# A 2-layer streaming encoder step: the first norm by sums over loaded rows of x, applied while its modulation loads

## The chip, the core and the metric

The kernel runs on one core of a Trainium2 chip. A core has TensorE (PE in the profile: matrix products, transpositions), VectorE (DVE), ScalarE (ACT: function tables, scaled copies), GpSimd (POOL) and SyncE (SP), which here issues most loads. Each engine works through its own queue in order, and they wait for each other by semaphores. The metric is the device time of one execution in microseconds (us). All data is fp32.

## What is computed

A two-layer trunk over 256 prompt rows and 8 x 16 sample rows of width 1024 (384 rows together), conditioned by c, of which there are 9 rows (1 prompt, 8 samples). Cut to what matters here:

```
def rmsnorm(x, g):
    y = xf * lax.rsqrt(jnp.mean(xf * xf, axis=-1, keepdims=True) + EPS)
    return (y * g.astype(jnp.float32)).astype(x.dtype)
...
    for l in range(DEPTH):
        mod = (jax.nn.silu(c) @ w_ada[l] + b_ada[l]).reshape(c.shape[0], N_MOD, D_MODEL)[:, :, None, :]
        h = rmsnorm(x, norm_g[l, 0]) * (1.0 + mod[:, 1]) + mod[:, 0]
        x = x + FFN_RES * mod[:, 2] * rmsnorm(swiglu(h, ffn_w_in[l, 0], ffn_w_out[l, 0]), norm_g[l, 1])
        ...
        h, st = token_mixing(h, pos, past, w_in[l], b_forget[l], w_branch[l], w_out[l])
        ...
```

`swiglu(h)` is `(silu(h @ w_gate) * (h @ w_up)) @ w_down`; token mixing holds three attention branches. The change touches only the first `h` of layer 0.

## The kernel before

x is held turned: X and H are 128 partitions (a block of 128 channels) x 8 blocks (k) x 384 rows. Columns 0 to 255 are prompt rows, 256 to 383 sample rows. The rows are worked on as two groups of 192 (group 0 or "a", group 1 or "b").

At the start SP loads x as rows (QR), c and the identity (IDENT), the raw biases and norm gains (BGR), then the first four modulation weights ADA_FIRST (2 MB each: 256 columns of shift and 256 of scale, so two blocks k of H each) and with them the "quarters" of the first SwiGLU tile XIN (0.5 MB each: two blocks k of 512 columns), then constants (masks, rotary tables), then the first two tiles of the ring RING (L417; each waits for a modulation product that frees its place).

PE turns x with 24 transpositions in 6 groups (L652) through two PSUM banks; ACT copies each group into X (L1361). ACT and DVE form silu(c) in BIG (L1358, L1851), PE turns it (L657), DVE copies it to CT (L1853). ACT squares X (L1371, 16 instructions), DVE adds the squares of the 8 blocks (L1867, 14), and a matmul with ONES (L663, function `mean`) gives every partition the sum of each row; ACT makes the reciprocal root from it by Ln and Exp (L1377, L1378).

The first modulation and the first product are four stages (`first_quarters` on PE, `first_norm` on DVE, `modulate_prompt` on ACT). In stage a: PE multiplies CT with ADA_FIRST[a] (L669, `ada_unit`), DVE copies the sums to AR (L1926), PE transposes AR (L676, `ada_turned`), DVE adds the bias (L2167), forms the scale (L2172), multiplies X with the norm and, for sample columns, with scale and shift (L2176 to L2184), and ACT scales and shifts the prompt columns (L1387). `quarter(q)` multiplies H's blocks 2q and 2q+1 with quarter q of XIN (L693, 8 matmuls); PE runs quarter(a-1) behind modulation a. Its sums feed the first two of 22 column tiles of the SwiGLU; the others follow as one long run (L727), for which DVE forms sums of weights and of H. Nothing else sets the order: it is written out in each engine's program.

Of the kernel before, what the change touches and what calls it, by code (L numbers as in the profile page):

```python
# [21 lines left out]
P = 128  # L22
# [139 lines left out]
def program(nc, t):  # L162
    with ExitStack() as ctx:
# [73 lines left out]
        BGR = [big(8192 + i * P, P) for i in range(DEPTH)]  # L237
        XIN = QKTR[:, 0:KD * 512].rearrange("p (k w) -> p k w", w=512)
# [72 lines left out]
        in_x, in_c, in_k, in_id = sem("in_x"), sem("in_c"), sem("in_k"), sem("in_id")  # L311
        c_act, c_silu, c_ready, ct_ready = sem("c_act"), sem("c_silu"), sem("c_ready"), sem("ct_ready")
        xt_ready, xt_free, x_turned = sem("xt_ready"), sem("xt_free"), sem("x_turned")
# [26 lines left out]
        bf_full, gc_full, gn_full = sem("bf_full"), sem("gc_full"), sem("gn_full")  # L340
# [23 lines left out]
        out_ready, out_stored = sem("out_ready"), sem("out_stored")  # L364
# [33 lines left out]
        def _(sp):  # L398
            sp.dma_start(qr(0, 2048).rearrange("p (t d) -> p t d", t=2),
                         t["x_prompt"].rearrange("o (t p) d -> p (o t) d", p=P)).then_inc(in_x, 16)  # L400
            sp.dma_start(qr(2048, 1024), t["x_sample"].rearrange("b t d -> (b t) d")).then_inc(in_x, 16)
            sp.dma_start(BIG[0:1, 0:D], t["c_prompt"]).then_inc(in_c, 16)
            sp.dma_start(BIG[1:NC, 0:D], t["c_sample"]).then_inc(in_c, 16)
            sp.dma_start(IDENT[:, :], t["k_ident"]).then_inc(in_id, 16)
            for l in range(DEPTH):
                sp.dma_start(BGR[l][0:72, :], t["b_ada"][l].rearrange("(m p) -> m p", p=P)).then_inc(bg_full, 16)
                sp.dma_start(BGR[l][72:120, :], t["norm_g"][l].rearrange("n (k p) -> (n k) p", p=P)).then_inc(bg_full, 16)

# [112 lines left out]
            sp.dma_start(MASKS, t["k_masks"]).then_inc(in_k, 16)  # L521
# [2030 lines left out]
```

## Time and profile before

| | us |
|---|---|
| median of 3 runs | 2334.58 |
| lowest, highest | 2334.51, 2334.95 |
| profiled execution, its time | 2335.47 |
| profiled execution, its span | 2333.6 |

The span runs from the first to the last recorded instruction; the rest of the execution's time lies around it. Engines' shares of the span: PE 98% (its weight loads 88%), DVE 53%, ACT 24%, POOL 0%. DMA moved 390.10 MB. All of it comes from one profiled execution. A wait in it is named by the engine that sat idle and by what released it; a time "from the start" is from the start of the span. An fp32 matmul that is not a transposition leaves two records.

### The profile page before, as it was taken

What the parts mean: (1) busy time and instruction counts of PE and PEld (TensorE: products, weight loads), DVE (VectorE), ACT (ScalarE), POOL (GpSimd) and SP (SyncE); (2) the same over time, 40 slices, a digit from 0 to 9 for tenths busy, and PEclk for the clock granted to TensorE, in tenths of its full rate; (3) what the DMA queues carried; (4) which work ended last, traced back from release to release, by engine and by line L of the source; (5) the groups of instructions that cost most, each with busy time, mean ns of one, the idle gap of its engine ahead of it and who ended that gap; (6) DMA issues with size and microseconds to landing.
All of it is one profiled execution on the core that took longest, in us unless ns stands there. A gap on an engine that the chain in (4) does not pass through costs nothing.

```text
span 2333.6 us, 41217 instructions
## 1 busy us (share of the span) xinstructions
PE 2297.0 (98%) x16916; PEld 2049.9 (88%) x16916; DVE 1231.9 (53%) x2700; ACT 556.3 (24%) x1349; POOL 68.8 (3%) x112
## 2 busy tenths in 40 slices
PE   7999999999999999999999999999999999999998
PEld 5999997886688699999999999978856886999998
DVE  5566433543656446666275664426345754666742
ACT  3000113113564231001130010321235642400011
POOL 0000000000022000000000000000000220000000
PEclk9999999999999999999999999999999999999999
DMA  9455234783489453443435533447825984233232
GB/s 337 136 176 176 96 127 152 232 263 103 149 286 343 138 191 111 145 145 100 136 127 178 177 131 116 167 132 237 261 68 189 333 290 149 73 109 109 100 122 77
DMA packets 300509, 390.10 MB, mean 167 GB/s; under 512 B 31005, under 2 KB 251033, under 8 KB 300322
## 3 DMA queue, kind: packets, MB, share of 16 engines
q1 hardware_dynamic: 281090, 336.41, 42.9%
q0 software_dynamic: 11712, 42.18, 5.2%
q10 hardware_dynamic: 7520, 8.87, 1.1%
q8 instruction: 135, 2.21, 0.4%
q14 instruction: 52, 0.43, 0.1%
HBM read 375.30 MB, written 12.12 MB: 166 GB/s over the span
## 4 chain that ended last, share of the span: by engine, by line
PE 94%; DMA 2%; ACT 2%; SPq 1%; DVE 1%; issue 1%; ACTq 0%; DVEq 0%
PE PS L727 31%; PE PS L823 13%; PE PS L1013 6%; PE PS L961 4%; PE PS L1281 4%; PE PS L910 4%; PE PS L669 3%; PE PS L1099 3%; PE PS L1180 3%; PE PS L871 2%; PE PS L983 2%; PE PS L879 2%; PE PS L1313 2%; PE PS L1321 2%; PE PS L1220 2%; PE PS L1195 1%
## 5 line engine op out<-in xcount | busy, mean ns | idle before, releaser
L727 PE MATMUL PS<-OT,RING 128*128 128x192 f32 x1280 | 234.1, 326 | 0.0
L727 PE MATMUL PS<-H,RING 128*128 128x192 f32 x1280 | 222.1, 327 | 0.0
L727 PE MATMUL PS<-OT,QR 128*128 128x192 f32 x1280 | 221.1, 326 | 0.0
L727 PEld LDWEIGHTS PS<-OT,RING 128*128 128x128 f32 x1280 | 212.4, 190 | 0.0
L727 PEld LDWEIGHTS PS<-H,RING 128*128 128x128 f32 x1280 | 208.4, 190 | 3.8 <-issue 3.2
L727 PEld LDWEIGHTS PS<-OT,QR 128*128 128x128 f32 x1280 | 210.2, 190 | 0.0
L1425 ACT ACTIVATE QR<-QR 128x384 f32<-128x384 f32 x80 | 41.8, 522 | 533.8 <-DVE QR L2011 533.8
L1013 PE MATMUL PS<-H,RING 128*128 128x384 f32 x480 | 161.1, 490 | 0.0
L1013 PEld LDWEIGHTS PS<-H,RING 128*128 128x128 f32 x480 | 88.9, 190 | 60.2 <-issue 3.7
L727 PE MATMUL PS<-H,QR 128*128 128x192 f32 x640 | 117.1, 326 | 0.0
L1867 DVE TENSOR_TENSOR OT<-OT 128x192 f32<-128x192 f32 x168 | 57.7, 354 | 105.7 <-ACT OT L1396 93.6
L727 PEld LDWEIGHTS PS<-H,QR 128*128 128x128 f32 x640 | 106.2, 190 | 0.0
L2011 DVE TENSOR_TENSOR QR<-PS,QR 128x384 f32<-128x384 f32 x80 | 44.6, 557 | 111.0 <-PE PS L727 111.0
L1281 PE MATMUL PS<-OT,RING 128*128 128x384 f32 x288 | 94.4, 487 | 0.0
L910 PE MATMUL PS<-RING,H 128*128 128x384 f32 (+1 forms) x288 | 90.3, 471 | 0.0
L823 PE MATMUL PS<-BIG,RING 128*128 128x192 f32 x528 | 89.7, 326 | 0.0
L2063 DVE TENSOR_TENSOR QR<-RING 128x768 f32<-128x768 f32 (+1 forms) x24 | 21.4, 890 | 124.3 <-DMA RING<-ffn_w_out 124.3
L823 PEld LDWEIGHTS PS<-BIG,RING 128*128 128x128 f32 x528 | 86.5, 190 | 0.0
L2006 DVE TENSOR_TENSOR QR<-PS,QR 128x384 f32<-128x384 f32 x80 | 44.4, 555 | 79.6 <-PE PS L727 79.6
L1281 PEld LDWEIGHTS PS<-OT,RING 128*128 128x128 f32 x288 | 54.1, 190 | 36.1
L910 PEld LDWEIGHTS PS<-RING,H 128*128 128x128 f32 x288 | 54.2, 190 | 32.2 <-issue 0.8
L983 PE MATMUL PS<-RING,H 128*128 128x384 f32 x224 | 74.5, 486 | 0.0
(325 smaller groups left out, 4005.7 us busy)
## 6 DMA issues: line engine op xcount, KB each, us to landing
RING<-ffn_w_in SPq DMA_DIRECT2D x80, 1024.0 KB, 7.2
RING<-w_in SPq DMA_DIRECT2D x64, 768.0 KB, 6.4
QR<-w_ada SPq DMA_DIRECT2D x34, 1024.0 KB, 9.7
BIG<-w_ada SPq DMA_DIRECT2D x34, 1024.0 KB, 10.6
RING<-ffn_w_out SPq DMA_DIRECT2D x32, 768.0 KB, 4.7
RING<-ffn_w_out SPq DMA_DIRECT2D x32, 640.0 KB, 5.4
QR<-cache_sb_v POOLq DMA_DIRECT2D x16, 768.0 KB, 5.3
QKT<-cache_sb_k SPq DMA_DIRECT2D x16, 768.0 KB, 5.7
```

The source lines that it names most:

```text
L669: mm = pe.matmul(PS[32 * j:32 * j + 32, bank, col:col + P], CT[:, k, :], w[:, k, j * P:(j + 1) * P], start=(k == 0), stop=(k == KD - 1))
L727: mm = pe.matmul(PS[:, bank, GROUP[g]], a[:, k, :], x[:, k, :], start=(k == 0), stop=(k == 3))
L823: mm = pe.matmul(PS[:, bank, 0:HALF], a[:, k, :], x[:, k, :], start=(half == 0 and k == 0), stop=(half == 1 and k == kn - 1))
L871: mm = pe.matmul(PS[:, m, 0:HALF], w[:, k, m * P:(m + 1) * P], HID[:, half * k2 + k, GROUP[0]], start=(half == 0 and k == 0), stop=(half = ...
L910: mm = pe.matmul(PS[:, n % 3, 0:width], H[:, k, tt * P:(tt + 1) * P], w[:, k, :], start=(k == 0), stop=(k == KD - 1))
L961: mm = pe.matmul(PS[:, bank, GROUP[half]], a[:, k, :], x[:, k, :], start=(k == 0), stop=(k == 3))
L983: mm = pe.matmul(PS[:, 4, 0:MIX], H[:, k, 2 * P:T], w[:, k, :], start=(k == 0), stop=(k == KD - 1))
L1013: mm = pe.matmul(PS[:, bank, 0:T], w[:, k, (n % 3) * P:(n % 3 + 1) * P], H[:, k, :], start=(k == 0), stop=(k == KD - 1))
L1099: mm = pe.transpose(PS[:, bank, c * P:(c + 1) * P], KC[:, n % KBUF, c, a * P:(a + 1) * P], IDENT[:, :])
L1180: mm = pe.matmul(PS[:, 3, 0:HALF], w[:, k, (n % 3) * P:(n % 3 + 1) * P], H[:, k, GROUP[half]], start=(k == 0), stop=(k == KD - 1))
L1281: mm = pe.matmul(PS[:, 3 * (m % 2) + n, 0:T], w[:, 3 * n + k, m * P:(m + 1) * P], OT[:, 3 * n + k, :], start=(k == 0), stop=(k == NPAIR - 1))
L1867: V.tensor_tensor(SQ[:, 0, GROUP[g]], SQ[:, 0, GROUP[g]], SQ[:, k, GROUP[g]], ALU.add).then_inc(sq_added[g], 1)
```

## The change

- **Loads.** x comes in three loads with a semaphore each. c (now as 72 rows of 128: `C0`), the identity, the biases and gains are issued by ACT, behind its table load. The first ADA_FIRST load is split by k into halves, each with its own wait inside `ada_unit`; quarters 2 and 3 of XIN move each behind its modulation weights; the constants move behind the first two ring tiles.
- **silu(c)** is Exp on ACT, then on DVE an addition, a reciprocal and a product on 72 x 128; one transposition turns it.
- **The norm.** ACT squares the loaded rows (`Square` with a running sum over the row, three instructions of 1024 columns), makes the reciprocal root of the 384 sums in 3 columns, DVE puts them on diagonals (DIAG, 128 x 384), and one matmul with ONES spreads them over all partitions in PSUM. DVE multiplies X with that, 4 instructions of 768 columns into H, ahead of the first modulation's copy AR. The old squares, additions, means and roots of this norm go; semaphores are advanced for them.
- **Copies of turned x** go from ACT to DVE.
- **PE** runs filling matmuls `warm(n)` on ONES, and `quarter(a)` now stands behind modulation a, not a+1.
- **Stage work.** DVE multiplies and adds the sample columns only; ACT scales 256 prompt columns in one instruction per block.

The semaphores' declarations, the body of `constants()` and the moved bias transposition and copy are left out of the diff.

```diff
@@ -396,15 +401,9 @@
 
         @block.sync
         def _(sp):
-            sp.dma_start(qr(0, 2048).rearrange("p (t d) -> p t d", t=2),
-                         t["x_prompt"].rearrange("o (t p) d -> p (o t) d", p=P)).then_inc(in_x, 16)
-            sp.dma_start(qr(2048, 1024), t["x_sample"].rearrange("b t d -> (b t) d")).then_inc(in_x, 16)
-            sp.dma_start(BIG[0:1, 0:D], t["c_prompt"]).then_inc(in_c, 16)
-            sp.dma_start(BIG[1:NC, 0:D], t["c_sample"]).then_inc(in_c, 16)
-            sp.dma_start(IDENT[:, :], t["k_ident"]).then_inc(in_id, 16)
-            for l in range(DEPTH):
-                sp.dma_start(BGR[l][0:72, :], t["b_ada"][l].rearrange("(m p) -> m p", p=P)).then_inc(bg_full, 16)
-                sp.dma_start(BGR[l][72:120, :], t["norm_g"][l].rearrange("n (k p) -> (n k) p", p=P)).then_inc(bg_full, 16)
+            for i in range(2):
+                sp.dma_start(qr(i * D, D), t["x_prompt"][0, i * P:(i + 1) * P, :]).then_inc(in_x[i], 16)
+            sp.dma_start(qr(2 * D, D), t["x_sample"].rearrange("b t d -> (b t) d")).then_inc(in_x[2], 16)
...
             for a in range(N_ADA_FIRST):
-                for i in range(2):
-                    sp.dma_start(ADA_FIRST[a][:, :, i * 256:(i + 1) * 256],
-                                 w[:, :, i * D + a * 256:i * D + (a + 1) * 256]).then_inc(first_full[a], 16)
-                for q in ((0,), (1,), (), (2, 3))[a]:
+                for h in range(2 if a == 0 else 1):
+                    ks = slice(4 * h, 4 * h + 4) if a == 0 else slice(0, KD)
+                    for i in range(2):
+                        sp.dma_start(ADA_FIRST[a][:, ks, i * 256:(i + 1) * 256],
+                                     w[:, ks, i * D + a * 256:i * D + (a + 1) * 256]).then_inc(
+                                         (first_full[0], second_half)[h] if a == 0 else first_full[a], 16)
+                for q in ((0,), (1,), (2,), (3,))[a]:
                     for dst, src in ffn_in(0, 0, XIN, 0):
                         sp.dma_start(dst[:, 2 * q:2 * q + 2, :], src[:, 2 * q:2 * q + 2, :]).then_inc(quarter_full[q], 16)
...
+            def warm(n):
+
+                for _ in range(n):
+                    pe.matmul(PS[:, 7, 0:P], ONES[:, :], ONES[:, :], start=True, stop=True)
+
+            def turned_in(g):
                 pe.wait_ge(xt_free, g + 1)
                 for j in range(4):
                     k, tt = 4 * (g % 2) + j, g // 2
                     mm = pe.transpose(PS[:, g % 2, j * P:(j + 1) * P],
                                       qr(tt * 1024 + k * P, P), IDENT[:, :])
                 mm.then_inc(xt_ready, 1)
+
+            pe.wait_ge(ones_ready, 1)
+            warm(6)
+            pe.wait_ge(in_id, 16)
+            for tt in range(TT):
+                pe.wait_ge(in_x[tt], 16)
+                turned_in(2 * tt)
+                turned_in(2 * tt + 1)
             pe.wait_ge(c_ready, 1)
-            for k in range(KD):
-                mm = pe.transpose(PS[:, 2, k * NC:(k + 1) * NC], BIG[0:NC, 3 * D + k * P:3 * D + (k + 1) * P], IDENT[0:NC, 0:NC])
-            mm.then_inc(ct_ready, 1)
+            pe.transpose(PS[:, 2, 0:KD * NC], C0, IDENT[0:KD * NC, 0:KD * NC]).then_inc(ct_ready, 1)
+            pe.wait_ge(bg_full, 64)
+            for i in range(DEPTH):
+                mm = pe.transpose(PS[:, 4, i * P:i * P + 120], BGR[i][0:120, :], IDENT[0:120, 0:120])
+            mm.then_inc(bg_ready, 1)
+            warm(4)
+            pe.wait_ge(diag_ready, 1)
+            pe.matmul(PS[:, 6, 0:T], ONES[:, :], OTR[:, D:D + T], start=True, stop=True).then_inc(ms_ready[0], 1)
+            warm(8)
             pe.wait_ge(c_silu, 1)
 
             def mean(q, g):
                 pe.wait_ge(sq_added[g], 7 * q + 7)
                 pe.matmul(PS[:, 6 + g, 0:HALF], ONES[:, :], SQ[:, 0, GROUP[g]], start=True, stop=True).then_inc(ms_ready[g], 1)
 
...
-            def ada_unit(w, bank=6, col=0):
+            def ada_unit(w, bank=6, col=0, halves=None):
 
                 for k in range(KD):
+                    if halves and k % 4 == 0:
+                        pe.wait_ge(halves[k // 4], 32)
                     for j in range(4):
                         mm = pe.matmul(PS[32 * j:32 * j + 32, bank, col:col + P], CT[:, k, :], w[:, k, j * P:(j + 1) * P],
                                        start=(k == 0), stop=(k == KD - 1))
...
-                    ada_unit(ADA_FIRST[a], 3)
+                    if a:
+                        pe.wait_ge(first_full[a], 32)
+                        ada_unit(ADA_FIRST[a], 3)
+                    else:
+                        ada_unit(ADA_FIRST[a], 3, halves=(first_full[0], second_half))
                     ada_turned(a, 0)
                     if a == 0:
-                        for g in range(2):
-                            mean(0, g)
-                    else:
-                        quarter(a - 1)
-                quarter(N_ADA_FIRST - 1)
+                        warm(6)
+                    quarter(a)
                 pe.wait_ge(mod_free, N_ADA_FIRST + 1)
 
...
+            nc.scalar.preload_act_table_set("natural_log_exp_and_others")
+            act.dma_start(BIG[0:KD, 0:P], t["c_prompt"].rearrange("o (k p) -> (o k) p", p=P)).then_inc(in_c, 16)
+            act.dma_start(BIG[KD:KD * NC, 0:P], t["c_sample"].rearrange("b (k p) -> (b k) p", p=P)).then_inc(in_c, 16)
+            act.dma_start(IDENT[:, :], t["k_ident"]).then_inc(in_id, 16)
+            for l in range(DEPTH):
+                act.dma_start(BGR[l][0:72, :], t["b_ada"][l].rearrange("(m p) -> m p", p=P)).then_inc(bg_full, 16)
+                act.dma_start(BGR[l][72:120, :], t["norm_g"][l].rearrange("n (k p) -> (n k) p", p=P)).then_inc(bg_full, 16)
+            begin()
             act.wait_ge(in_c, 32)
...
+            A(C1, C0, ACT.Exp, scale=-1.0).then_inc(c_act, 1)
+            for tt in range(TT):
+                act.wait_ge(in_x[tt], 16)
+                link(A(XSQ, qr(tt * D, D), ACT.Square, accum_out=XSUM[:, tt:tt + 1]))
+            act.wait_ge(ones_ready, 1)
+            link(A(XRSTD, XSUM, ACT.Ln, scale=1.0 / D, bias=EPSC[:, :]))
+            A(XRSTD, XRSTD, ACT.Exp, scale=-0.5).then_inc(rstd_ready[0], 1)
 
             def squares_of_x(e, g, ks):
 
...
+            for k in range(KD):
+                act.wait_ge(coef_ready, k // 2 + 1)
+                act.wait_ge(hs_ready[0], k // 2 * 2 + 2)
+                h = H[:, k, 0:NPROMPT]
+                A(h, h, ACT.Identity, scale=MOD[0][:, KD + k, 0:1], bias=MOD[0][:, k, 0:1]).then_inc(h_ready[0], 1)
 
...
+            def taken_in(g):
+
+                dve.wait_ge(xt_ready, g + 1)
+                V.tensor_copy(X[:, 4 * (g % 2):4 * (g % 2) + 4, (g // 2) * P:(g // 2 + 1) * P],
+                              PS[:, g % 2, :].rearrange("p (k t) -> p k t", k=4)).then_inc(xt_free, 1)
+
+            taken_in(0)
+            taken_in(1)
             dve.wait_ge(c_act, 1)
-            c, e, g = (BIG[0:NC, i * D:(i + 1) * D] for i in (0, 1, 3))
-            V.tensor_tensor(g, c, e, ALU.mult).then_inc(c_ready, 1)
+            link(V.tensor_scalar(C2, C1, 1.0, None, ALU.add))
+            link(V.reciprocal(C1, C2))
+            V.tensor_tensor(C0, C0, C1, ALU.mult).then_inc(c_ready, 1)
+            for g in range(2, 6):
+                taken_in(g)
             dve.wait_ge(ct_ready, 1)
-            link(V.tensor_copy(CT[:, :, 0:NC], PS[:, 2, 0:KD * NC].rearrange("p (k c) -> p k c", c=NC)))
+            link(V.tensor_copy(CT[:, :, 0:NC].rearrange("p k c -> p c k"), PS[:, 2, 0:KD * NC].rearrange("p (c k) -> p c k", c=NC)))
             link(V.tensor_copy(ROWS[:, :].rearrange("p (z t) -> p z t", z=2), IDENT[:, 0:NT][:, None, :].to_broadcast([P, 2, NT])))
             dve.sem_inc(c_silu, 1)
-            dve.wait_ge(x_turned, 1)
-            for g in range(2):
-                dve.sem_inc(x_ready[g], KD)
+            dve.wait_ge(rstd_ready[0], 1)
+            V.tensor_tensor(DIAG, IDENT[:, :][:, None, :].to_broadcast([P, TT, P]), XRSTD[..., None].to_broadcast([P, TT, P]),
+                            ALU.mult).then_inc(diag_ready, 1)
+            dve.wait_ge(bg_ready, 1)
+            for i in range(DEPTH):
+                ins = V.tensor_copy(BG[i][:, :], PS[:, 4, i * P:i * P + 120])
+            ins.then_inc(bg_free, 1)
+            dve.wait_ge(xt_free, 2 + 6)
+            dve.wait_ge(ms_ready[0], 1)
+            for q in range(N_ADA_FIRST):
+                k = slice(2 * q, 2 * q + 2)
+                V.tensor_tensor(H[:, k, :], X[:, k, :], PS[:, 6, 0:T][:, None, :].to_broadcast([P, 2, T]), ALU.mult).then_inc(hs_ready[0], 2)
 
             def add_squares(q, g, ks):
...
                 dve.sem_inc(coef_ready, 1)
-                for g in range(2):
-                    dve.wait_ge(rstd_ready[g], 1)
-                link(V.tensor_tensor(sample_cols(H)[:, k], sample_cols(X)[:, k], per_sample(0, KD)[:, k], ALU.mult))
-                for i in (2 * q, 2 * q + 1):
-                    V.tensor_tensor(H[:, i, 0:HALF], X[:, i, 0:HALF], RSTD[:, 0:HALF], ALU.mult).then_inc(hs_ready[0], 1)
-                V.tensor_tensor(H[:, k, HALF:NPROMPT], X[:, k, HALF:NPROMPT],
-                                RSTD[:, HALF:NPROMPT][:, None, :].to_broadcast([P, 2, NPROMPT - HALF]), ALU.mult)
-                link(V.tensor_tensor(H[:, k, NPROMPT:T], H[:, k, NPROMPT:T],
-                                     RSTD[:, NPROMPT:T][:, None, :].to_broadcast([P, 2, NSAMPLE]), ALU.mult))
+                dve.wait_ge(hs_ready[0], 2 * q + 2)
                 hs = sample_cols(H)[:, k]
-                V.tensor_tensor(hs, hs, per_sample(0, 0)[:, k], ALU.add).then_inc(hs_ready[1], 2)
+                link(V.tensor_tensor(hs, hs, per_sample(0, KD)[:, k], ALU.mult))
+                V.tensor_tensor(hs, hs, per_sample(0, 0)[:, k], ALU.add).then_inc(h_ready[1], 2)
 
             for q in range(N_ADA_FIRST):
```

PE, from the first transposition to the second stage's quarter, before (QR holds x, BIG c and the raw biases, CT silu(c), RING and QR later modulation weights, QKT the tile XIN):

```order
L652 MATMUL PS<-IDENT,QR 128x128 x24
L657 MATMUL PS<-IDENT,BIG 128x9 x8
L892 MATMUL PS<-IDENT,BIG 128x120 x2
L669 MATMUL PS<-RING,CT 32x128 x32
L676 MATMUL PS<-IDENT,AR 128x128
L663 MATMUL PS<-OT,ONES 128x192 x2
L669 MATMUL PS<-RING,CT 32x128 x32
L676 MATMUL PS<-IDENT,AR 128x128
L693 MATMUL PS<-H,QKT 128x384 x8
```

and after:

```order
L662 MATMUL PS<-IDENT,QR 128x128 x24
L674 MATMUL PS<-IDENT,BIG 128x72
L677 MATMUL PS<-IDENT,BIG 128x120 x2
L656 MATMUL PS<-ONES 128x128 x4
L681 MATMUL PS<-OT,ONES 128x384
L656 MATMUL PS<-ONES 128x128 x8
L695 MATMUL PS<-RING,CT 32x128 x32
L702 MATMUL PS<-IDENT,AR 128x128
L656 MATMUL PS<-ONES 128x128 x6
L719 MATMUL PS<-H,QKT 128x384 x8
L695 MATMUL PS<-RING,CT 32x128 x32
```

The spreading matmul (L681) stands ahead of the first modulation product, and the first quarter ahead of the second one.

DVE, from the silu of c to the end of the first stage, before:

```order
L1851 TENSOR_TENSOR BIG<-BIG 9x1024
L1853 COPY CT<-PS 128x8x9
L1854 COPY ROWS<-IDENT 128x32
L2156 COPY BG<-PS 128x120 x2
L1867 TENSOR_TENSOR OT<-OT 128x192 x14
L1926 COPY AR<-PS 128x128
```

and after, from the first copies of turned x on:

```order
L1881 COPY X<-PS 128x4x128 x2
L1887 TENSOR_SCALAR BIG<-BIG 72x128
L1888 RECIPROCAL BIG<-BIG 72x128
L1889 TENSOR_TENSOR BIG<-BIG 72x128
L1881 COPY X<-PS 128x4x128 x4
L1893 COPY CT<-PS 128x9x8
L1894 COPY ROWS<-IDENT 128x32
L1897 TENSOR_TENSOR OT<-IDENT,ST 128x384
L1901 COPY BG<-PS 128x120 x2
L1907 TENSOR_TENSOR H<-X,PS 128x768 x4
L1975 COPY AR<-PS 128x128
```

Fourteen additions leave the place ahead of AR, and four products of 768 columns, six copies and the diagonal take it.

## Rows read from the trace of the kernel before

**Rows 1.** The page, part 1: busy us, share of the span, instructions.

```profile
PE 2297.0 (98%) x16916; PEld 2049.9 (88%) x16916; DVE 1231.9 (53%) x2700; ACT 556.3 (24%) x1349; POOL 68.8 (3%) x112
```

**Rows 2.** The page, part 4: the chain that ended last, by engine.

```profile
PE 94%; DMA 2%; ACT 2%; SPq 1%; DVE 1%; issue 1%; ACTq 0%; DVEq 0%
```

**Rows 3.** Waits of PE, 0 to 100 us: total, times, longest.

```profile
PE PS L652 <- DMA IDENT<-k_ident: 8.1, 1, 8.1
PE PS L676 <- DVE AR L1926: 5.1, 4, 3.5
```

**Rows 4.** Timeline from the start: start, us, engine, line, operation [idle before].

```profile
0.73 1.28 ACT L1358 ACT_TABLE_LOAD   x1 [0.73 <-PEq L2544]
...
2.42 0.37 SPq L404 DMA_DIRECT2D IDENT<-k_ident  x1
...
8.09 5.09 PE L652 MATMUL PS<-IDENT,QR 128*128 128x128 f32 x24 [8.09 <-DMA IDENT<-k_ident]
...
9.21 0.60 ACT L1361 ACTIVATE X<-PS 128x512 f32<-128x512 f32 x1 [0.42 <-PE PS L652]
...
13.80 0.23 DVE L1853 COPY CT<-PS 128x72 f32<-128x72 f32 x1 [3.69 <-PE PS L657]
...
14.37 0.42 PE L892 MATMUL PS<-IDENT,BIG 120*128 120x120 f32 x2 [0.60 <-DVEq L1855]
...
15.35 3.53 PE L669 MATMUL PS<-RING,CT 128*32 128x128 f32 x64 [0.56 <-DVE BG L2156]
...
22.04 0.28 DVE L1926 COPY AR<-PS 128x128 f32<-128x128 f32 x1
```

**Rows 5.** Timeline of the third stage, and where the long run begins.

```profile
33.33 1.95 PE L669 MATMUL PS<-QR,CT 128*32 128x128 f32 x64
...
35.35 0.29 DVE L1926 COPY AR<-PS 128x128 f32<-128x128 f32 x1 [4.62 <-PE PS L669]
...
35.70 0.33 PE L676 MATMUL PS<-IDENT,AR 128*128 128x128 f32 x1 [0.41 <-DVE AR L1926]
...
35.87 5.33 PE L693 MATMUL PS<-H,QKT 128*128 128x384 f32 x16
36.07 0.20 DVE L2167 TENSOR_TENSOR MOD<-PS,BG 128x36 f32<-128x36 f32 x1 [0.42 <-PE PS L676]
...
36.70 0.43 DVE L2176 TENSOR_TENSOR H<-X,MOD 128x256 f32<-128x256 f32 x1 [0.22 <-DVE MOD L2172]
...
37.61 0.98 ACT L1387 ACTIVATE H<-H,MOD 128x192 f32<-128x192 f32 x2 [6.01 <-DVE H L2178]
...
41.13 1.69 PEld L669 LDWEIGHTS PS<-BIG,CT 128*32 128x32 f32 x64 [0.55 <-issue]
...
53.99 5.36 PE L727 MATMUL PS<-H,RING 128*128 128x192 f32 x32
```

**Rows 6.** DMA issues: count, KB each, median us from issue to landing.

```profile
IDENT<-k_ident SPq DMA_DIRECT2D x1, 64.0 KB, 5.6
...
o_y_p<-QR ACTq DMA_DIRECT2D x4, 256.0 KB, 2.0
```

**Rows 7.** Groups by line and shape: busy us, mean ns | idle before.

```profile
L2420 DVE COPY NORM<-PS 128x512 f32<-128x512 f32 x24 | 16.3, 681 | 0.0
...
L1979 DVE TENSOR_TENSOR OT<-H 128x768 f32<-128x768 f32 x4 | 3.8, 951 | 0.0
...
L2428 DVE RECIPROCAL ST<-ST 128x1 f32<-128x1 f32 x24 | 3.7, 153 | 0.0
...
L2386 DVE RECIPROCAL ST<-ST 128x6 f32<-128x6 f32 x8 | 1.5, 192 | 12.3 <-ACT QR L1652 12.0
...
L1647 ACT ACTIVATE QR<-QR 128x768 f32<-128x768 f32 x4 | 3.4, 844 | 0.1
```

**Rows 8.** Windows: us, PE busy (instructions), granted clock, DMA share, GB/s.

```profile
15.00:19.00 4.00, 3.53 (x64) 0.57 1.09 386
27.00:28.00 1.00, 0.33 (x1) 1.00 1.10 354
```

More of the change, by code:

```diff
@@ L237, in program @@
         BGR = [big(8192 + i * P, P) for i in range(DEPTH)]
+        C0, C1, C2 = (BIG[0:KD * NC, i * P:(i + 1) * P] for i in range(3))
+        XSQ, DIAG = OTR[:, 0:D], OTR[:, D:D + T].rearrange("p (t c) -> p t c", t=TT)
+        XSUM, XRSTD = ST[:, 0:TT], ST[:, 8:8 + TT]
         XIN = QKTR[:, 0:KD * 512].rearrange("p (k w) -> p k w", w=512)
@@ L308, in sems @@
             return [sem(f"{name}_{g}") for g in "ab"]
-        in_x, in_c, in_k, in_id = sem("in_x"), sem("in_c"), sem("in_k"), sem("in_id")
+        in_x = [sem(f"in_x{i}") for i in range(TT)]
+        in_c, in_k, in_id = sem("in_c"), sem("in_k"), sem("in_id")
         c_act, c_silu, c_ready, ct_ready = sem("c_act"), sem("c_silu"), sem("c_ready"), sem("ct_ready")
-        xt_ready, xt_free, x_turned = sem("xt_ready"), sem("xt_free"), sem("x_turned")
+        ones_ready, diag_ready = sem("ones_ready"), sem("diag_ready")
+        xt_ready, xt_free, second_half = sem("xt_ready"), sem("xt_free"), sem("first_second_half")
         settled = sem("settled")
@@ L643, in full @@
                 pe.wait_ge(slot_full[n % 2], 32 * (n // 2 + 1))
-            pe.wait_ge(in_x, 32)
-            pe.wait_ge(in_id, 16)
-            for g in range(6):
+            def warm(n):
+                for _ in range(n):
+                    pe.matmul(PS[:, 7, 0:P], ONES[:, :], ONES[:, :], start=True, stop=True)
+            def turned_in(g):
                 pe.wait_ge(xt_free, g + 1)
@@ L888, in swiglu_out @@
                         mm.then_inc(half_used, 1)
-            pe.wait_ge(bg_full, 64)
-            for i in range(DEPTH):
-                mm = pe.transpose(PS[:, 3, i * P:i * P + 120], BGR[i][0:120, :], IDENT[0:120, 0:120])
-            mm.then_inc(bg_ready, 1)
-            pe.wait_ge(bg_free, 2)
             for l in range(DEPTH):
@@ L1383, in modulate_prompt @@
                 for k in ks:
-                    act.wait_ge(coef_ready, COEF_NORM[e] if e else k // 2 + 1)
+                    act.wait_ge(coef_ready, COEF_NORM[e])
                     act.wait_ge(hs_ready[g], 8 * e + k + 1)
@@ L1844, in _ @@
             link(V.memset(EPSC[:, :], EPS))
-            link(V.memset(ZERO[:, :], 0.0))
-            link(V.memset(QBLK, 0.0))
-            link(V.memset(CT, 0.0))
-            dve.wait_ge(c_act, 1)
-            c, e, g = (BIG[0:NC, i * D:(i + 1) * D] for i in (0, 1, 3))
-            V.tensor_tensor(g, c, e, ALU.mult).then_inc(c_ready, 1)
+            dve.sem_inc(ones_ready, 1)
+            for g in range(2):
+                for s, n in ((sq_ready[g], KD), (sq_added[g], KD - 1), (x_ready[g], KD)):
+                    dve.sem_inc(s, n)
@@ new lines, in _ @@
+            for s, n in ((ms_ready[1], 1), (rstd_ready[1], 1), (hs_ready[1], KD)):
+                dve.sem_inc(s, n)
+            link(V.memset(CT, 0.0))
+            link(V.memset(ZERO[:, :], 0.0))
+            def taken_in(g):
[3 more added lines that the diff above has]
+            taken_in(0)
@@ new lines, in _ @@
+            dve.wait_ge(bg_ready, 1)
+            for i in range(DEPTH):
+                ins = V.tensor_copy(BG[i][:, :], PS[:, 4, i * P:i * P + 120])
[5 more added lines that the diff above has]
+                V.tensor_tensor(H[:, k, :], X[:, k, :], PS[:, 6, 0:T][:, None, :].to_broadcast([P, 2, T]), ALU.mult).then_inc(hs_ready[0], 2)
@@ L2152, in choose @@
                     link(V.match_replace(WK[qt], M8, WK[qt], TAKEN))
-            dve.wait_ge(bg_ready, 1)
-            for i in range(DEPTH):
-                ins = V.tensor_copy(BG[i][:, :], PS[:, 3, i * P:i * P + 120])
-            ins.then_inc(bg_free, 1)
             dve.wait_ge(bg_free, 2)
```

40 lines of the change are left out of this document (11 added, 29 removed).

## The prediction

> **What bounds the kernel now.** I read the page first: TensorE (PE) is busy 98% of the span [rows 1], and the chain that ended last is 94% PE, 2% DMA, 2% ScalarE (ACT) [rows 2]. So the change can only matter where PE waits. The waits of the first 100 us say where that is in the edited part: 8.1 us until the identity matrix has landed, and 5.1 us in total (3.5 us the longest) for VectorE's (DVE's) copy AR [rows 3]. The timeline shows the order [rows 4]: PE turns x from 8.09, the silu of c is ready with the copy at 13.80, the first modulation product (L669, 64 records) starts at 15.35, and its copy AR only starts at 22.04, because DVE adds squares until then. From 33.33 there is no such wait; one stage is shown in [rows 5]: modulation product 33.33, AR 35.35, its transposition 35.70, and at 35.87 a quarter of the first SwiGLU product (L693), which belongs to the modulation before this one. So DVE and ACT prepare H (from 36.07 on) under that quarter, and PE is never idle for it. At 53.99 the long solid stretch (L727) begins. After that row nothing is edited that PE waits for; the change is worth what it moves 53.99, and all else shifts with it.
>
> **How long one stage becomes.** The order rows show that quarter q now stands right behind modulation q and its transposition, where before quarter q-1 stood. Everything between transposition and H is then in PE's way. From [rows 5]: the transposition starts at 35.70, the bias addition at 36.07, then the scale, and the first product with H at 36.70, so 1.00 us. That product (0.43) stays for the sample columns; the addition behind it (0.43) follows at a distance of 0.11, as for other dependent pairs on DVE; 0.1 for the semaphore: 1.00 + 0.43 + 0.11 + 0.43 + 0.1 = 2.07 us from transposition to quarter, where 0.17 stood. ACT's two modulations of 256 columns run beside it from about 0.95 on; two of 192 take 0.98 [rows 5], so they end at the same place. The products of x with the norm no longer stand here: they were DVE's and hidden; that removal is worth 0 in these stages. One stage: 2.02 (33.33 to 35.35) + 0.35 + 2.07 + 5.26 (35.87 to 41.13) = 9.70 us. Of four stages the last has no product behind it: 38.8 us from the first modulation product to L727. Before, it is 53.99 - 15.35 = 38.6 us, with the 3.5 us wait and half-clock stretches in it. So what is gained at the first wait is spent in four new ones, and **L727 moves by about what the first modulation product moves** (15.2 is the even point).
>
> **Where the first modulation product goes.** It needs its weights, c, and in PE's order now also the mean of squares and eight filling matmuls. Weights: they were there at 15.35, and the halves come no later. The rest hangs on the identity's landing I. Before: issued 2.42, landed 8.0 [rows 4, 6]. Now ACT issues it behind its table load and two loads of c, at about 2.7 (table load 0.73 + 1.28, two issues of some 0.35 as SP's). Bounds for the landing are 5.6 us and 2.0 us, the quickest landing in the trace, a store from ACT's queue at the end [rows 6]: I = 4.7 to 8.3. I take 6.3, since it stands behind no megabyte on its queue but shares the DMA engines with x.
>
> The Trainium skill, "DMA: Bandwidth & Descriptors", section "Issuing engines are not separate DMA queues", says that issues of several engines interleave on the same 16 DMA engines and that spreading them saves only issue time; this speaks against the change. No row before has two queues busy at the start. By that rule I would be 8.3, and the sum below 2.0 us more; that is rival D.
>
> From I on, DVE is the longest chain. First copy of turned x 1.1 later (8.09 to 9.21 [rows 4]); six copies of 512 from PSUM at 0.68 [rows 7] (ACT did them before) = 4.1; silu by three operations on 72x128 between the second and the third: addition 0.25, product 0.28, and a reciprocal, whose rows give 153 ns for 1 column and 192 for 6, so 7.8 ns a column and 1.14 for 128 [rows 7], with gaps 1.95 in all; waits for two banks 0.7 (four transpositions 0.8 and the way there are longer than one copy); CT 0.23 [rows 4], ROWS less than that, diagonal of 384 columns some 0.55, gaps 0.4. Together 1.1 + 8.1 = 9.2. ACT's three squares of 1024 columns (some 1.1 each, from 844 ns for 768 [rows 7]) end before that: cost 0. The bias transpositions, two, lie in PE's pauses: 0. On PE then the mean, one matmul of 384 columns, is an eighth of a quarter (5.26 us), 0.65; eight fills of 128 columns 8 x 0.215 = 1.7. First modulation product: 6.3 + 9.2 + 0.65 + 1.7 + 0.05 = **17.9**, against an even point of 15.2: **+2.7 us**. DVE's four new products of 768 columns (4 x 0.95 [rows 7], 3.75) start with the mean's end, 16.2, and end at 20.0, just as the modulation product (1.95) does: no more cost, but none to spare. What was removed here (16 squares, 14 additions, four root steps) is in the 38.6 and so counted.
>
> **The clock.** PE at half clock: from 15 to 19 the granted clock is 0.57 on average, that is at its lower level (1.2 of 2.4 GHz) for most of it, after light work (two small transpositions at 14.37, pauses on both sides [rows 4]); such a stretch costs 4 x (1 - 0.57) = 1.7 us of PE work [rows 8]. A gap of 0.7 us with one transposition (27 to 28) brought no fall [rows 8]. Start: if the mean, the fills or the modulation product fall into a stretch at half clock, up to 1.7 is added; I add 0.8: **+3.5**. Stages: each has 0.4 idle, one transposition of 0.33, then 1.74 idle (the first filled by six matmuls). That is more idle than the case that fell and less than the wait of 3.5 us. I take one fall in the three unfilled gaps: +1.7, bounds 0 and 5.1.
>
> **Other edits.** Constants of 1 MB move behind the two ring loads: used only at the projections, cost 0; the ring loads are earlier. DMA: each stage needs 2.6 MB at 354 to 386 GB/s [rows 8], 7 us in 9.7: hidden, and the split of the first load and of the quarters gives nothing once the product starts at 17.9. The memset of QBLK was under the loads: 0. ACT's second table load (1.28 [rows 4]) goes, off the path that now decides. DVE's sums behind the last quarter: four of 512 columns at about 0.7 and four of 768 at 0.95, 6.6 us, beside 5.2 us of quarter and 5 us of L727 products that need only H: hidden by 3 us.
>
> **Sum.** 2335.47 us of the profiled execution (span 2333.6) + 3.5 + 1.7 = 2340.7; the profiled execution is 0.9 over the median of 2334.58, so 2339.8 on the scale of the medians.
>
> **The rivals.**
> A, the forecast: start +3.5 and one or more falls of the clock, 2339.8 (2338.5 to 2343). For it: the gap nearest in kind fell. 0.45.
> B, no fall in the gaps: 2338.1 (2336.5 to 2339.5). For it: the gap at 27; PE is at work 7.5 of 9.7 us. 0.25.
> C, not slower: the small loads on ACT's queue land at once (I = 4.7) and the silu slips between copies that wait anyway (0.7 and 1.0 less): product at 14.6, 0.6 us under the even point, 2334.0; with the loads alone early 16.3, 2335.7. It decides from a product start below 15.2. Against it: DVE's nine copies and products in a row. 0.15.
> D, the identity waits behind x as before (I = 8.3): +5.5 without a fall, +7.2 with one: 2340.1 to 2341.8. 0.12.
> E, clearly faster: needs the product before 10.6 or a stage without its gap. The first is excluded by the weights (2.1 MB behind 1.6 MB of x) and the second by the waits for H. 0.03 for what I overlook.
>
> **How the numbers follow.** A measurement of this kernel tells 0.2% (4.7 us, above 2339.25) from no change. Slower: most of A (0.42), D 0.12 and a little of B: 0.55. Same: the rest of A, B and C: 0.42. Faster 0.03. The likeliest case gives 2339.8; the range 2335.5 to 2342.5 leaves out the early half of C, E, and starts with three falls.
>
> **What would show it.** Right: the first modulation product starts at 16.3 to 19.9; behind each of the four AR transpositions PE is idle or filling for about 1.7 us until H, released by DVE's sample addition or ACT; stages of 9.7 us; L727 from 56.7 to 61; half-clock slices behind one or two gaps; identical waits after that. The reciprocal takes about 1.1 us. Wrong: stages of 7.9 us, a product before 15, L727 before 54, or a change of more than 1 us behind L727's start.

## The result, and the profile after

| | before | changed |
|---|---|---|
| median, us | 2334.43 (7 runs, 2333.78 to 2334.95) | 2341.90 (7 runs, 2340.15 to 2343.38) |
| ratio to before, 95% interval | | 1.0030 (1.0020 to 1.0039) |
| profiled execution, time and span | 2335.47, 2333.6 | 2341.90, 2340.1 |

The change makes the kernel slower by 7.5 us. The forecast was 2339.8 with a range of 2335.5 to 2342.5, and slower with a chance of 0.55. The medians lie 7.5 us apart, the two profiled executions 6.4.

The timeline of the changed kernel up to the first quarter (start, us, engine, line, operation [idle before, what ended it]); compare [rows 4]:

```profile
2.04 0.60 ACTq L1380 DMA_DIRECT2D IDENT<-k_ident  x1
...
8.17 4.00 PE L662 MATMUL PS<-IDENT,QR 128*128 128x128 f32 x16 [2.43 <-DMA IDENT<-k_ident]
...
11.03 0.95 DVE L1888 RECIPROCAL BIG<-BIG 72x128 f32<-72x128 f32 x1
...
13.05 1.16 PE L662 MATMUL PS<-IDENT,QR 128*128 128x128 f32 x8 [0.87 <-DVE X L1881]
...
14.32 1.06 PE L656 MATMUL PS<-ONES 128*128 128x128 f32 x8
...
16.17 0.91 PE L681 MATMUL PS<-OT,ONES 128*128 128x384 f32 x2 [0.79 <-DVE OT L1897]
...
16.92 1.95 PE L656 MATMUL PS<-ONES 128*128 128x128 f32 x16
17.23 3.55 DVE L1907 TENSOR_TENSOR H<-X,PS 128x768 f32<-128x768 f32 x4 [0.73 <-PE PS L681]
18.80 1.96 PE L695 MATMUL PS<-RING,CT 128*32 128x128 f32 x64
...
21.24 0.33 PE L702 MATMUL PS<-IDENT,AR 128*128 128x128 f32 x1 [0.49 <-DVE AR L1975]
...
23.67 5.40 PE L719 MATMUL PS<-H,QKT 128*128 128x384 f32 x16 [0.76 <-DVE H L2222]
```

The 3.5 us wait for AR is gone (0.49 is left), and the first quarter starts at 23.67 where it started at 28.00. But the first modulation product starts at 18.80 where it started at 15.35. Then one stage and the start of the long run, against [rows 5]:

```profile
29.00 1.95 PE L695 MATMUL PS<-RING,CT 128*32 128x128 f32 x64
...
31.02 0.29 DVE L1975 COPY AR<-PS 128x128 f32<-128x128 f32 x1 [7.50 <-PE PS L695]
31.37 0.33 PE L702 MATMUL PS<-IDENT,AR 128*128 128x128 f32 x1 [0.41 <-DVE AR L1975]
...
32.23 1.09 ACT L1495 ACTIVATE H<-H,MOD 128x256 f32<-128x256 f32 x2 [9.03 <-DVEq L2218]
32.29 0.42 DVE L2221 TENSOR_TENSOR H<-H,MOD 128x256 f32<-128x256 f32 x1
32.83 0.42 DVE L2222 TENSOR_TENSOR H<-H,MOD 128x256 f32<-128x256 f32 x1
...
33.40 5.40 PE L719 MATMUL PS<-H,QKT 128*128 128x384 f32 x16 [1.70 <-ACT H L1495]
38.72 1.95 PE L695 MATMUL PS<-QR,CT 128*32 128x128 f32 x64
...
43.12 6.94 PE L719 MATMUL PS<-H,QKT 128*128 128x384 f32 x16 [1.70 <-ACT H L1495]
...
59.62 5.36 PE L753 MATMUL PS<-H,RING 128*128 128x192 f32 x32
```

From transposition to quarter it is 33.40 - 31.37 = 2.03 us, where 0.17 stood; a stage is 38.72 - 29.00 = 9.72 us, where it was 7.8. One quarter took 6.94 us instead of 5.40. The windows (us, PE busy, granted clock, DMA share, GB/s) say why: the granted clock fell to its lower level (1.2 GHz) for a part of the first window. Nothing of the kind came with the last gap:

```profile
42.00:47.00 5.00, 3.88 (x8) 0.66 1.09 397
51.00:54.00 3.00, 1.27 (x37) 1.00 0.23 29
```

The long run starts 5.6 us later than before. The waits of PE in the first 100 us (total, times, longest), against [rows 3]:

```profile
PE PS L719 <- ACT H L1495: 5.1, 3, 1.7
PE PS L662 <- DMA IDENT<-k_ident: 2.4, 1, 2.4
PE PS L702 <- DVE AR L1975: 1.7, 4, 0.5
```

Behind the long run's start the two traces run alike for a long way. One solid piece of PE work of 75.08 us (L823 before, L849 after), which comes back several times, starts at 249.32, 1075.25 and 1397.51 before, and at 254.94, 1080.79 and 1403.05 after, always 5.5 to 5.6 later. The missing 0.9 us up to the spans' difference of 6.5 arose after 1403, in the second layer, where nothing was edited. It need not be a cost of the change: the span behind the long run's start is 2279.6 us here before and 2280.5 after, and it was 2278.0 in a second profiled execution of the same changed kernel.

### The profile page after: what moved, and what is told of

The parts are those of the page before. It is cut to its first block, busy times and chain, and to the rows that moved or that the text cites. A ratio compares the mean times of both kernels' runs of the same rounds, so it can differ in the third digit from the quotient of the medians.

```text
span 2340.1 us, 41239 instructions
## 1 busy us (share of the span) xinstructions
PE 2302.4 (98%) x16955; PEld 2054.2 (88%) x16955; DVE 1228.0 (52%) x2682; ACT 546.8 (23%) x1322; POOL 68.8 (3%) x112
## 4 chain that ended last, share of the span: by engine, by line
PE 94%; ACT 2%; SPq 2%; DMA 1%; DVE 1%; issue 1%; ACTq 0%; DVEq 0%
PE PS L753 31%; PE PS L849 13%; PE PS L1033 6%; PE PS L1301 4%; PE PS L981 4%; PE PS L930 4%; PE PS L695 3%; PE PS L1119 3%; PE PS L1200 3%; PE PS L897 2%; PE PS L1003 2%; PE PS L905 2%; PE PS L1333 2%; PE PS L1341 2%; PE PS L1240 2%; PE PS L1215 1%
## 5 line engine op out<-in xcount | busy, mean ns | idle before, releaser
L1916 DVE TENSOR_TENSOR OT<-OT 128x192 f32<-128x192 f32 x154 | 52.7, 352 | 103.8 <-ACT OT L1423 93.6
L849 PE MATMUL PS<-BIG,RING 128*128 128x192 f32 x528 | 89.7, 326 | 0.0
L849 PEld LDWEIGHTS PS<-BIG,RING 128*128 128x128 f32 x528 | 86.5, 190 | 0.0
```

Of the source, the lines that this page charges most:

```text
L849: mm = pe.matmul(PS[:, bank, 0:HALF], a[:, k, :], x[:, k, :], start=(half == 0 and k == 0), stop=(half == 1 and k == kn - 1))
L1916: V.tensor_tensor(SQ[:, 0, GROUP[g]], SQ[:, 0, GROUP[g]], SQ[:, k, GROUP[g]], ALU.add).then_inc(sq_added[g], 1)
```

## The experiments

The first four experiments ran on one chip, the next four on a second, the last two on a third; each ratio is to runs of the kernel before on the same chip and has a 95% interval. Times are medians. Two kernels were run in two sets each; their distance to the kernel before differed by 0.6 and 1.0 us between the sets, so a difference between experiments of different sets is no finer than that.

**The order of the quarters undone.** The one edit to the changed kernel:

```diff
                     ada_turned(a, 0)
-                    if a == 0:
-                        warm(6)
-                    quarter(a)
+                    if a:
+                        quarter(a - 1)
+                quarter(N_ADA_FIRST - 1)
```

> The changed kernel with one thing undone: quarter(a-1) stands behind modulation a again, as before the change; new norm, loads and copies stay. Theory (the order exposes the way from each AR transposition to H, about 1.9 us in each of four stages, and this ate the gain of the new norm): PE has no wait for H; the first modulation product stays at 18.8 us, the first quarter comes at about 24.1, stages of 7.8 us follow, and the long run starts at about 50 us where the changed kernel has 59.6 and the one before 54.0. Time 2330.5 to 2332.5 us. Rival (the new norm and the later start of the first modulation product are what costs, the order little): long run at 57 to 58, time 2339 to 2341 us.

Measured: 2332.95 us against 2334.72, ratio 0.9991 (0.9982 to 1.0000); 9 us under the changed kernel. The profiled execution's waits for H are gone and the stage is 7.8 us again:

```profile
20.37 1.96 PE L695 MATMUL PS<-RING,CT 128*32 128x128 f32 x64
...
25.65 5.40 PE L719 MATMUL PS<-H,QKT 128*128 128x384 f32 x16
30.98 1.95 PE L695 MATMUL PS<-QR,CT 128*32 128x128 f32 x64
33.35 0.33 PE L702 MATMUL PS<-IDENT,AR 128*128 128x128 f32 x1 [0.41 <-DVE AR L1975]
33.51 5.33 PE L719 MATMUL PS<-H,QKT 128*128 128x384 f32 x16
38.78 1.96 PE L695 MATMUL PS<-BIG,CT 128*32 128x128 f32 x64
...
51.64 5.36 PE L753 MATMUL PS<-H,RING 128*128 128x192 f32 x32
```

The start of this execution was late by itself: the identity landed at 9.0 and the work up to the product took 0.7 us longer, so the first modulation product started at 20.37, not 18.80, and the long run at 51.64 instead of 50. (The changed kernel's second profile, below, has the same late start.) From first modulation product to long run it is 31.3 us, where the changed kernel has 40.8 (39.3 without its fall of the clock) and the one before 38.6. So the order alone costs 8 us, and the rival that gave it little has fallen. What else was edited makes the kernel 1.8 us faster than before at the most likely, and the interval reaches 1.0000. The time is 0.5 us above the expected range; this execution also lost 3.5 us to before between 247 and 1076 us, 1.6 of it in a single longer wait for a later modulation weight (2.0 instead of 0.4); the rest I can't place.

**The order alone.** The kernel before, with one edit:

```diff
                         for g in range(2):
                             mean(0, g)
-                    else:
-                        quarter(a - 1)
-                quarter(N_ADA_FIRST - 1)
+                    quarter(a)
```

> The kernel before with one thing changed: quarter(a) stands behind modulation a, all else as before. Theory (exposed way to H): here the products of x with the norm and the 64-column modulations stand in that way too, so it is about 4.0 us a stage (35.70 to 39.72 in the trace of before, and 0.1); first quarter at 28.3, stages of 11.8, long run at about 68.7 instead of 54.0: 2349 us, up to 2354 if the clock falls in each gap. Rival (order costs little): 2334 to 2337 us.

Measured: 2357.19 us, ratio 1.0095 (1.0080 to 1.0111), 22 us slower and 3 above the range. The last two stages:

```profile
51.11 0.33 PE L676 MATMUL PS<-IDENT,AR 128*128 128x128 f32 x1 [0.41 <-DVE AR L1924]
54.94 7.90 PE L693 MATMUL PS<-H,QKT 128*128 128x384 f32 x16 [3.51 <-ACT H L1385]
62.77 1.95 PE L669 MATMUL PS<-BIG,CT 128*32 128x128 f32 x64
65.14 0.33 PE L676 MATMUL PS<-IDENT,AR 128*128 128x128 f32 x1 [0.41 <-DVE AR L1924]
...
75.90 4.39 PE L725 MATMUL PS<-H,RING 128*128 128x192 f32 x26
```

The exposed way is 54.94 - 51.11 = 3.83 us a stage (4.0 expected). Without falls the long run would start at 27.73 + 3 x 11.5 + 5.2 = 67.4; it started at 75.90. Of the 8.5 us between them 8.3 are the clock's (stage: 1.96 + 0.41 + 3.83 + 5.3 = 11.5): the four quarters took 7.85, 7.09, 7.90 and 7.09 us instead of 5.40. So behind a gap of 3.8 us every quarter ran partly at half clock, and a fall cost up to 2.5 us, not 1.7 at most. With the new norm the order costs 9 us, with the old one 22. Read the other way, the new norm, loads and fills together save 15 us in the new order (2357.2 to 2341.9) and under 2 in the old one (2334.7 to 2333.0), where the work that they take out of the stages was hidden.

**Fills in every gap.** Six filling matmuls stand behind each AR transposition, not behind the first alone:

```diff
                     ada_turned(a, 0)
-                    if a == 0:
-                        warm(6)
+                    warm(6)
                     quarter(a)
```

> The changed kernel with the six filling matmuls (about 1.3 us of PE work) behind the AR transposition of every stage, not of the first alone. Theory (one fall of the clock in some runs' gaps, none in others, two in others): no slice at half clock between 21 us and the long run, which starts at about 58.0 instead of 59.6; median about 2340.3 us, and the runs lie within about 1.3 us of each other where the changed kernel's lie within 3.2. Rival (the spread and the level have another cause): median 2341.9 and a spread of 3 us as before, or longer where the fills are themselves late for H.

Measured: 2340.52 us, ratio 1.0025 (1.0016 to 1.0034). The median came out as expected, though the interval overlaps the changed kernel's. The profiled execution has no slice below full clock in the stages. Its long run starts at 59.85, not at 58.0, because the first modulation product started only at 20.56; from product to long run it is 39.3 us, as in the changed kernel without its fall. The spread did not shrink: 11 runs lie between 2337.8 and 2344.2, and 21 runs of the kernel before on this chip between 2333.3 and 2337.7. So the spread is not that of the falls. The profiles show two other sources, the start (product at 18.80 to 20.56) and the waits far behind it; how much each gives was not measured. The gap itself stays, now filled:

```profile
42.86 0.33 PE L702 MATMUL PS<-IDENT,AR 128*128 128x128 f32 x1 [0.41 <-DVE AR L1974]
43.02 1.50 PE L656 MATMUL PS<-ONES 128*128 128x128 f32 x12
44.89 5.40 PE L719 MATMUL PS<-H,QKT 128*128 128x384 f32 x16 [0.36 <-ACT H L1494]
```

**No fills at all.** All 24 filling matmuls of the changed kernel are left out:

```diff
-            pe.wait_ge(ones_ready, 1)
-            warm(6)
...
-            warm(4)
...
-            warm(8)
...
-                    if a == 0:
-                        warm(6)
```

> The changed kernel without any filling matmul. Theory (DVE's chain of the six copies, the silu and the four norm products sets the first AR copy at 20.9, the eight fills ahead of the first modulation product cost nothing beyond it, but keep the clock up): the product starts at about 17.1, AR at 20.9 at full clock or 21.5 to 22 at half clock, and gaps fall as often or oftener; 2341.5 to 2345 us. Rival (the fills themselves stand in the way): 1.7 us faster, 2340.2.

Measured: 2345.62 us, ratio 1.0044 (1.0031 to 1.0056), 0.6 above the range and 3.7 us slower than with them; the rival has fallen. In the profiled execution the identity landed at 8.2 as in the changed kernel's first profile. The first modulation product starts a microsecond earlier than there and ends later, because it runs at 1.2 GHz, and two of the four quarters meet a fall, the first among them, whose six fills are gone too:

```profile
17.80 3.64 PE L691 MATMUL PS<-RING,CT 128*32 128x128 f32 x64
21.94 0.48 PE L698 MATMUL PS<-IDENT,AR 128*128 128x128 f32 x1 [0.49 <-DVE AR L1969]
24.51 7.09 PE L715 MATMUL PS<-H,QKT 128*128 128x384 f32 x16 [2.09 <-DVE H L2216]
```

**The changed kernel again, and with the identity first.** The second of the two has the identity as SyncE's first load:

```diff
         def _(sp):
+            sp.dma_start(IDENT[:, :], t["k_ident"]).then_inc(in_id, 16)
...
-            act.dma_start(IDENT[:, :], t["k_ident"]).then_inc(in_id, 16)
```

> The changed kernel once more, nothing edited, as the measure for the next run on the same chip. The identity (issued on ScalarE's queue at 2.0 us) lands at 8 to 9 us, the first modulation product starts at 18.8 to 19.7, one or two falls of the clock in the three unfilled gaps: 2340 to 2343 us.

Measured: 2341.78 us, ratio 1.0029 (1.0018 to 1.0040): the result again, in another set of runs. Its profile differs from the first in three places:

```profile
8.82 4.01 PE L662 MATMUL PS<-IDENT,QR 128*128 128x128 f32 x16 [3.08 <-DMA IDENT<-k_ident]
13.70 1.94 PE L662 MATMUL PS<-IDENT,QR 128*128 128x128 f32 x8 [0.87 <-DVE X L1881]
...
15.95 1.93 PE L656 MATMUL PS<-ONES 128*128 128x128 f32 x8
...
20.41 1.96 PE L695 MATMUL PS<-RING,CT 128*32 128x128 f32 x64
...
35.00 7.09 PE L719 MATMUL PS<-H,QKT 128*128 128x384 f32 x16 [1.70 <-ACT H L1495]
...
61.38 5.36 PE L753 MATMUL PS<-H,RING 128*128 128x192 f32 x32
```

The identity landed 0.65 us later. The last transpositions of x took 1.94 us instead of 1.16 and the four fills 1.93 instead of 1.06, so PE was still at 1.2 GHz there, where in the first profile it was at 2.4 GHz from 13 us on (the windows print a granted clock of 1.00 here; the trace has no clock record ahead of the first rise, and the durations decide). From the landing to the first modulation product it is 1.0 us more for it (11.6 instead of 10.6). That product therefore starts at 20.41, 0.7 above the expected 19.7, and the long run 7.4 us later than before the change, not 5.6. The fall of the clock stands in another gap, ahead of the second quarter instead of the third. Three of the four profiles of kernels with this start have the product at 20.4 to 20.6 (the first experiment, the third and this one), so the first profile was an early one. Why the clock rises late in them is not shown.

> The changed kernel with the identity as SyncE's first load, ahead of x, instead of ScalarE's third. Theory (small loads on ScalarE's queue share the DMA engines with x and land as late as behind it; the identity's landing starts the whole chain): the first transposition waits for x's first rows instead, at about 5.6 us, the first modulation product and the long run are 2 to 2.5 us earlier than in the changed kernel, time lower by as much, 2339.5 us. Rival (the chain hangs on the silu of c, which lands at 6.9, or on the last rows of x): less than 1 us.

Measured: 2338.04 us, ratio 1.0015 (1.0006 to 1.0025), 3.7 us faster than the changed kernel beside it. PE's first transposition follows the fills without a wait for the identity:

```profile
0.74 0.39 SPq L404 DMA_DIRECT2D IDENT<-k_ident  x1
...
5.53 1.22 PE L663 MATMUL PS<-IDENT,QR 128*128 128x128 f32 x8
...
15.65 1.95 PE L696 MATMUL PS<-RING,CT 128*32 128x128 f32 x64
```

The identity landed 1.8 us after its issue. The modulation product starts at 15.65, 4.8 us earlier than in the profile of the changed kernel beside it and 3.2 earlier than in the first one; the long run starts at 56.62 instead of 61.38. So the chain hung on the identity, and more than the expected 2 to 2.5 us; the rival (less than 1 us) has fallen. Even so the kernel is 3.2 us slower than before: with the product at its old place, the exposed gaps and one fall are left.

**Norm products spread.** On top of the old order: in DVE's program one norm product stands ahead of the first AR copy, and each other behind the coefficients of the stage before; the eight fills ahead of the first modulation product are gone.

```diff
-            for q in range(N_ADA_FIRST):
+            def normed(q):
+
                 k = slice(2 * q, 2 * q + 2)
                 V.tensor_tensor(H[:, k, :], X[:, k, :], PS[:, 6, 0:T][:, None, :].to_broadcast([P, 2, T]), ALU.mult).then_inc(hs_ready[0], 2)
+
+            normed(0)
...
                 ada_rows(q, 3)
                 first_norm(q)
+                if q + 1 < N_ADA_FIRST:
+                    normed(q + 1)
```

> The old order of quarters as in the first experiment, and in addition the norm's four products of 768 columns spread: the first ahead of the first AR copy, each other behind the coefficients of the stage before; the eight fills ahead of the first modulation product are left out. Theory (DVE's 3.5 us of products and the 1.7 us of fills are what stands between the mean and AR): AR transposition 1.8 us earlier (17.5 to 19.5 us at full clock against 21.2), long run at 48.5 to 50.5: 2331 us, 1.8 below the first experiment's; if the clock falls at the start, up to 1.7 of it is lost. Rival (the start is bound by the identity alone): as the first experiment, 2333.

Measured: 2331.26 us, ratio 0.9984 (0.9975 to 0.9992). It is faster than before by 3.6 us and than the first experiment by 1.7, as expected, but on another chip and with intervals that overlap. In the profiles the first AR transposition comes at 21.17 instead of 22.81 (17.5 to 19.5 was expected; the identity landed at 8.7 and the clock rose late here too), and the long run at 50.37 instead of 51.64. So the theory agrees with the traces, while the times alone do not show the gain; the spread products and the missing fills were not tried apart.

**Both together.** The kernel with spread norm products, and the identity as SyncE's first load, by the edits shown above.

> The kernel of the run before with the identity as SyncE's first load. Theory: both gains add, the long run at 46 to 48, 2328 to 2329.5 us, 5 to 6.5 below the kernel before. Rival (the DMA is then what is late: modulation weights of the second and third stage are waited for): 2330 to 2331.

Measured: 2333.87 us, ratio 0.9996 (0.9987 to 1.0005). It is 2.6 us slower than the run before, against the theory and beyond the rival, whose mechanism it shows:

```profile
16.76 0.33 PE L702 MATMUL PS<-IDENT,AR 128*128 128x128 f32 x1 [0.49 <-DVE AR L1977]
...
21.81 3.64 PE L695 MATMUL PS<-RING,CT 128*32 128x128 f32 x64 [4.72 <-DMA RING<-w_ada]
...
52.06 4.23 PE L753 MATMUL PS<-H,RING 128*128 128x192 f32 x25
```

The first modulation product starts at 14.31, 4.4 us earlier than in the run before. PE is ready for the second one at 17.1 and waits 4.7 us for its weights, until 21.81; in the run before that product started at 21.43 without a wait. So the weights arrive when they did, and the gain at the front is lost. Behind the wait the clock was at 1.2 GHz (granted 0.62 on average from 17 to 26 us), and the product took 3.64 us instead of 1.95; these 1.7 us are what the long run starts later (52.06 against 50.37).

**A version that uses that wait.** The kernel of "Both together" with `quarter(0)` right behind modulation 0 (six fills between), the others one stage behind, four fills behind the second transposition, and XIN's second quarter loaded behind the third modulation weights, its third with its fourth. The kernel with the norm products spread ran again beside it. The edit is shown against the changed kernel, without what is shown above:

```diff
-                for q in ((0,), (1,), (2,), (3,))[a]:
+                for q in ((0,), (), (1,), (2, 3))[a]:
...
                     if a == 0:
                         warm(6)
-                    quarter(a)
+                        quarter(0)
+                    if a == 1:
+                        warm(4)
+                    if a > 1:
+                        quarter(a - 1)
+                quarter(N_ADA_FIRST - 1)
```

> The kernel of the seventh experiment (old order, norm products spread, no eight fills) once more, nothing edited, as the measure for the next run on the same chip: 2330.5 to 2332 us, the long run at about 50.4 us.

Measured: 2332.14 us, ratio 0.9989 (0.9980 to 0.9998): 0.1 above the expected range, the long run at 49.92, and 2.6 us below the kernel before where it was 3.6 the first time. Over the first experiment (1.8 below) little of the gain is left.

> The kernel of the eighth experiment (identity first, norm products spread) with the first quarter right behind modulation 0, six fills between them, where PE waited 4.7 us for the second modulation weights, and the other quarters one stage behind as in the old order; four fills behind the second AR transposition; the second quarter's load stands behind the third modulation weights. Theory (an exposed gap to H costs nothing where PE would wait for weights anyway): first quarter at 18.8 us, second modulation product at 24.1 at full clock, third at 27.5 to 28.5 when its weights have landed, long run at 48.5 to 49.2: 1.2 to 1.9 us below the seventh experiment, 2329.3 to 2330. Rival (the third weights land later, or the clock falls behind the second transposition): no gain over the seventh.

Measured: 2329.74 us, ratio 0.9975 (0.9966 to 0.9985): 5.0 us below the kernel before, 2.4 below the run beside it and 12 below the change; both the time and the long run's start are as the theory has them. Its start:

```profile
14.88 1.96 PE L695 MATMUL PS<-RING,CT 128*32 128x128 f32 x64
...
19.35 5.40 PE L719 MATMUL PS<-H,QKT 128*128 128x384 f32 x16 [0.36 <-ACT H L1499]
24.68 1.96 PE L695 MATMUL PS<-RING,CT 128*32 128x128 f32 x64
...
48.86 5.36 PE L758 MATMUL PS<-H,RING 128*128 128x192 f32 x32
```

The first quarter and the gap ahead of it cost little here: they fill the time in which the version under "Both together" waited 4.7 us for the second weights, and that wait is gone.

## Why the prediction was right

**What bounds, and what the change is worth.** Right. The spans differ by 6.5 us, and 5.6 of it is the shift of the long run's start.

**The length of a stage.** Right nearly to the digit: 2.03 us from transposition to quarter (2.07 forecast), 9.72 a stage (9.70), and in both profiles. In the first stage it was 2.43, because DVE's addition started 0.5 us behind the product instead of 0.1. That this order costs 8 to 9 us against the old one was not said in the prediction, which set it against the old wait; the first experiment shows it.

**The first modulation product.** 17.9 forecast, 18.80 and 20.41 measured. This is the term that was mis-sized. The identity's landing was taken as 6.3; it was 8.2, and 8.6 to 9.0 in most other executions. I had set the rule of the Trainium skill ("DMA: Bandwidth & Descriptors", section "Issuing engines are not separate DMA queues") aside as rival D; the trace agrees with the rule, by which a second issuing engine saves only the time of the issue: issued at 2.04 on ScalarE's queue it needed 6.1 us, more than the 5.6 on SyncE's behind all of x [rows 6]. From there to the product it was 10.6 us in the first profile, 11.6 forecast, which took half of that error back: the silu took 1.35 us instead of 1.95 (its reciprocal 0.95 instead of 1.14), the waits for banks 0.2 instead of 0.7. In the second profile it was 11.6, but only because PE was at half clock for a part of it.

**The clock.** One fall, as forecast, for 1.5 us (1.7 forecast). It came in the second unfilled gap of three in one profile and in the first in another. That a fall is bounded at 1.7 is wrong, as the order alone shows (2.5). The 0.8 for the start was not needed in the first profile; in the second the half clock there cost 1.0.

**The sum.** For the long run 5.2 us were forecast; 5.6 and 7.4 were measured. The medians differ by 7.5 and, in the second set of runs, by 6.9, which fits the later start better. The rest of the execution moves by as much again without any edit in it: from the long run's start to the end it is 2280.5 us in one profile of the changed kernel and 2278.0 in the other, and 2279.6 before the change. So the 0.9 us behind the long run in the first pair of profiles can't be counted as a term that the prediction lacked. The forecast of 2339.8 was 2.1 us too low, about what the landing was missed by. The mechanism and the stages were right; that the range held the time all the same is owed to its upper end, which allowed for a late landing or more falls.

**The rivals.** D (landing 8.3, one fall of the clock) gives 2341.8 and comes closest to the measured 2341.90; the landings were 8.2 to 9.0. Its chance of 0.12 was too small. The fills in every gap are the case of B (no fall): they bring 1.4 us of its 1.7, but from the higher level, 2340.5, above B's range. C decided at a product start below 15.2: the run with the identity first reached 15.65, and its long run was 2.6 us behind that of the kernel before, 0.45 + 1.7 by the prediction and 0.5 more, so the even point was near enough.

## What to carry to other kernels

When a pipelined loop is rewritten so that the consumer stands right behind its own producer, add up everything between the producer's result and the consumer's operand; it is paid in every stage, and here (four times 1.9 us) it outweighed a removed wait of 3.5 us. Leave the consumer one stage behind, and put it right behind its producer only where the engine would wait for data anyway. A stall taken from the front is gained only as far as the loads behind it arrive earlier too.

## What the runs showed of the hardware

- A gap on TensorE of 0.4 us idle, one small transposition of 0.33 us and 1.7 us idle brought a fall from 2.4 to 1.2 GHz in one gap of three, in each of four profiled executions, and the quarter behind it took 6.9 to 7.1 us instead of 5.4. Gaps of 3.5 to 3.9 us idle brought one each time, with quarters of 7.1 to 7.9 us. Six filling matmuls in the gap (1.5 us) kept the clock up in the profiled execution.
- The same start of the same kernel reached full clock at about 13 us in one execution and only at about 18 us in another, with 0.65 us between the landings of the first operand.
- A reciprocal of 128 columns took 0.95 us on DVE, where a product of as many took 0.29.
- A load of 64 KB on ScalarE's queue, issued third there while SyncE's queue moved 1.5 MB, landed 6.1 to 6.9 us after its issue; on SyncE's queue behind those 1.5 MB it took 5.6, and as the first load there 1.8 to 2.0.
